# The third mixer of a two-network kernel, rearranged by head group

## What is computed

```python
def fox_attention(q, k, v, logf):                  # 16 heads of 64, 256 tokens
    c = jnp.cumsum(logf, axis=1).transpose(0, 2, 1)
    for i in range(nb):                            # two blocks of 128 queries
        lo, hi = i * blk, (i + 1) * blk
        s = einsum('bqhd,bkhd->bhqk', q[:, lo:hi], k[:, :hi]) * scale
        s = s + c[:, :, lo:hi, None] - c[:, :, None, :hi]
        p = softmax(where(causal, s, NEG_INF))
        outs.append(einsum('bhqk,bkhd->bqhd', p, v[:, :hi]))

def fox_mixer(h, w_in, b_f, w_out):
    q, k, v, fl = split(h @ w_in, [1024, 2048, 3072])   # fl: one logit a head
    logf = log_sigmoid(fl + b_f)
    return fox_attention(q, k, v, logf) @ w_out
```

## Time and profile before

| what | us |
|---|---|
| median of 3 timed runs (1780.7 to 1783.34) | 1781.23 |
| the profiled execution's own time | 1790.02 |
| its span, first to last instruction | 1788.3 |
| PE busy in the span | 1709.6 (96%) |
| DVE, ACT, POOL busy | 1080.5, 802.1, 163.6 |
| mixer: first product of the columns to first of the output product | 1434.01 to 1554.62 |

### The profile page before, as it was taken

The page is one execution under the profiler, slowest core; times in us unless marked ns, Lnnn a source line. Parts: engine busy times, 40 slices in busy tenths (PEclk is TensorE's granted clock), DMA queues, the critical chain, the costliest instruction groups (busy, mean ns, idle before and its releaser), DMA issues.

```text
span 1788.3 us, 31012 instructions
## 1 busy us (share of the span) xinstructions
PE 1709.6 (96%) x13150; PEld 1641.2 (92%) x13150; DVE 1080.5 (60%) x1060; ACT 802.1 (45%) x935; POOL 163.6 (9%) x123
## 2 busy tenths in 40 slices
PE   7999998999999999999999998889999999789997
PEld 7999985899999999989999998669999998689997
DVE  6564776465567664686556876555655566556553
ACT  5343557444346443464434544345444544444442
POOL 1000123100003000030000342110000000100000
PEclk9999999999999999999999998779999999999999
DMA  7544451164543644446454353003554525125550
GB/s 275 210 171 181 165 190 68 50 257 150 210 156 129 258 169 183 180 161 241 153 199 168 137 200 142 1 24 119 189 177 176 211 83 201 47 96 192 185 188 24
DMA packets 39636, 282.33 MB, mean 158 GB/s; under 512 B 4416, under 2 KB 4544, under 8 KB 5760
## 3 DMA queue, kind: packets, MB, share of 16 engines
q1 hardware_dynamic: 39168, 279.59, 42.2%
q0 software_dynamic: 384, 1.51, 0.2%
HBM read 280.03 MB, written 1.05 MB: 157 GB/s over the span
## 4 chain that ended last, share of the span: by engine, by line
PE 88%; DVE 5%; ACT 4%; DMA 1%; issue 1%; POOL 1%; SPq 0%; DVEq 0%; ACTq 0%; POOLq 0%
PE ps L308 27%; PE ps L309 27%; PE ps L310 27%; ACT arena L1078 1%; PE ps L662 1%; PE ps L392 1%; PE ps L606 1%; ACT w_hi L894 1%; DVE w_lo L1213 1%; DMA raw<-weights 1%; PE ps L619 1%; PE ps L638 0%; PE ps L663 0%; POOL arena L1825 0%; DVE stat L1523 0%
## 5 line engine op out<-in xcount | busy, mean ns | idle before, releaser
L308 PE MATMUL ps<-hT_hi,w_hi 128*128 128x256 f32 x2520 | 720.8, 286 | 25.5 <-DVE hT_lo L1225 18.9
L309 PE MATMUL ps<-hT_lo,w_hi 128*128 128x256 f32 x2520 | 716.4, 284 | 0.0
L310 PE MATMUL ps<-hT_hi,w_lo 128*128 128x256 f32 x2520 | 716.2, 284 | 0.0
L1213 DVE TENSOR_TENSOR w_lo<-raw,w_hi 128x2048 fp32r<-128x2048 f32 x264 | 601.0, 2299 | 147.1 <-ACT w_hi L894 147.0
L894 ACT ACTIVATE w_hi<-raw 128x2048 fp32r<-128x2048 f32 x264 | 494.7, 1902 | 62.7 <-DMA raw<-weights 50.8
L308 PEld LDWEIGHTS ps<-hT_hi,w_hi 128*128 128x128 f32 x2520 | 486.7, 193 | 28.3 <-DVE w_lo L1213 13.1
L309 PEld LDWEIGHTS ps<-hT_lo,w_hi 128*128 128x128 f32 x2520 | 487.2, 193 | 0.8 <-issue 0.7
L310 PEld LDWEIGHTS ps<-hT_hi,w_lo 128*128 128x128 f32 x2520 | 486.9, 193 | 0.0
L308 PE MATMUL ps<-hid_hi,w_hi 128*128 128x256 f32 x1256 | 356.0, 283 | 2.6 <-DVE hid_lo L1313 2.6
L309 PE MATMUL ps<-hid_lo,w_hi 128*128 128x256 f32 x1256 | 356.6, 284 | 0.0
L310 PE MATMUL ps<-hid_hi,w_lo 128*128 128x256 f32 x1256 | 351.7, 280 | 0.0
(11 more groups left out here) (227 smaller groups left out, 1468.1 us busy)
## 6 DMA issues: line engine op xcount, KB each, us to landing
raw<-weights SPq DMA_DIRECT2D x264, 1024.0 KB, 4.8
X<-x SPq DMA_DIRECT2D x2, 512.0 KB, 7.1
out<-X SPq DMA_DIRECT2D x4, 256.0 KB, 2.1
arena<-p POOLq DMA_DIRECT2D x2, 256.0 KB, 6.0
arena<-counts POOLq DMA_DIRECT2D x1, 512.0 KB, 4.6
arena<-nsa_tables POOLq DMA_DIRECT2D x1, 448.0 KB, 6.9
const<-constants SPq DMA_DIRECT2D x1, 423.0 KB, 10.0
cols<-parameters SPq DMA_DIRECT2D x1, 213.5 KB, 2.6
```

The lines of the kernel that those rows point to most:

```text
L308: nc.tensor.matmul(dst, a_hi, b_hi, start=start, stop=False, skip_group_check=True)
L309: nc.tensor.matmul(dst, a_hi, b_lo, start=False, stop=False, skip_group_check=True)
L310: return nc.tensor.matmul(dst, a_lo, b_hi, start=False, stop=stop, skip_group_check=True)
L1213: nc.vector.tensor_tensor(unit_cols(w_lo, u, 0, UNIT), raw[:, r * UNIT:(r + 1) * UNIT], f(unit_cols(w_hi, u, 0, UNIT)), ALU.subtract).then ...
```

## The change

The units of the mixer come in another order: the logits' unit first, then for each group of four heads one unit of Q, one of K, one of V (256 columns each), then the output product. PE runs them as `unit(0)` to `unit(11)`, each in a bank of its own among 4 to 7. Scores, transposes and weighted sums of a group are put between the products of later units, and those of the last group between products of the output. There is one score buffer now (banks 0 to 2, the transposes use them too) and one bank (3) for a group's result, which is kept aside once (`heads_aside`). V has the tokens stationary and 256 columns moving, in place of 512. ACT and DVE get a hand-written order to match.

The forget table is gone: the logits are laid down twice (rows 0 to 15 and 32 to 47), rows 32 to 63 of `FORGET` become the low half, and one product a head and tile with `PICK` adds both halves at once. Its moving sides are 256 and 128 columns.

```diff
@@ PE: fox @@
-                logits_and_columns(u0)
-                for b in range(1, 4):
-                    columns_t([u0 + 1 + 2 * b, u0 + 2 + 2 * b], mid={1: lambda: sums(s), 5: lambda: spread(7)} if b == 1 else {})
-                columns([u0 + 9, u0 + 10])
...
-                softmax_attention(FOX_JOBS, ..., prologue, v_ready)
-                project(u0 + 13, squares=True)
+                def scores(g):
+                    if g == 0:
+                        pe.wait_ge(*forget_split.due(me))
+                    pe.wait_ge(qk_taken.sem, 2 * g + 2)
+                    for s in range(HG):
+                        h = HG * g + SLOT_HEAD[s]
+                        pick = PICK[:, h:h + 1].broadcast_to((P, P))
+                        nc.tensor.matmul(A(0, s, 0, 256), pick, FORGET, start=s % 2 == 0, stop=False, skip_group_check=True)
+                        nc.tensor.matmul(bank(2, s * P, P), pick, FORGET[:, 0:P], start=s == 0, stop=False, skip_group_check=True)
...
+                def output(u):
+                    for k in range(KC):
+                        if k % 2 == 0:
+                            pe.wait_ge(hT_ready.sem, heads_before + k // 2 + 1)
+                        for m in range(KC):
+                            if (k, m) == (3, 6):
+                                transposed(3)
+                            elif (k, m) == (4, 3):
+                                weighted(3)
...
+                logits_and_first()
+                unit(1, {2: lambda: sums(s), 6: lambda: spread(7)})
+                unit(2, {7: forget_columns})
+                unit(3, {1: lambda: scores(0)})
+                unit(4)
+                unit(5, {4: lambda: transposed(0), 6: lambda: weighted(0), 7: lambda: scores(1)})
+                unit(6)
+                unit(7)
+                unit(8, {2: lambda: transposed(1), 4: lambda: weighted(1), 5: lambda: scores(2)})
+                unit(9)
+                unit(10)
+                unit(11, {0: lambda: transposed(2), 2: lambda: weighted(2), 3: lambda: scores(3)})
+                hT_ready.due(me, GROUPS)
+                pe.wait_ge(qk_taken.sem, 2 * GROUPS)
+                pe.wait_ge(v_taken.sem, GROUPS)
+                output(u0 + 13)
@@ ACT: fox, in its new order @@
+                split_to(u0 + 9)
+                values(0)
+                split_to(u0 + 10)
+                exponentials()
+                split_to(u0 + 12)
+                copy_transposed()
+                values(1)
+                heads_high(0)
+                split_to(u0 + 13)
+                exponentials()
+                split_to(u0 + 15)
+                copy_transposed()
+                values(2)
+                heads_aside()
...
+                copy_transposed()
+                split_to(u0 + 18)
+                values(3)
+                heads_high(1)
+                heads_high(2)
+                exponentials()
+                split_to(u0 + 19)
+                copy_transposed()
+                heads_high(3)
@@ DVE: fox, its first two groups @@
+                split_to(u0 + 8)
+                masked_scores(0)
+                columns_taken(3)
+                split_to(u0 + 10)
+                weights()
+                columns_taken(4)
+                copy_transposed()
+                split_to(u0 + 12)
+                heads_low(0)
+                masked_scores(1)
+                columns_taken(6)
+                split_to(u0 + 13)
+                weights()
+                columns_taken(7)
+                copy_transposed()
```

More of the change, by code:

```diff
@@ L81 @@
 NTABLE = 2 * TOKENS + 3 * P
-FOX_JOBS = [(g, "fox") for g in range(GROUPS)]
 NSA_JOBS = [(g, b) for g in range(GROUPS) for b in ("slc", "win", "cmp")]
@@ L141, in network_kernel @@
         cols = sb("cols", NCOLS)
-        stat = sb("stat", 192)
+        stat = sb("stat", 160)
         spare = sb("spare", 512)
@@ L207, in pooled_chunk, with heads_chunk @@
             return chunk(h, 2 * g + c, n) if g < 2 else chunk(hid, 2 * (g - 2) + c, n)
+        def heads_chunk(hid, h, k, n=1):
+            return chunk(hid if k < 2 else h, k, n)
         def lhs(t, c, tok):
@@ new lines, in fox, with values @@
+                act.wait_ge(*c_ready.due(me))
+                nc.scalar.activation(FORGET, MINUS_C, ACT.Copy).then_inc(forget_hi.sem, 1)
+                def values(g):
+                    act.wait_ge(unit_used.sem, u0 + 4 + 3 * g)
+                    for tok in range(TT):
+                        ins = nc.scalar.activation(at(QKV + 4096 + tok * DM + g * 256, 256), bank(4 + (3 * g + 2) % 4, tok * 256, 256), ACT.Copy, scale=rstd[:, tok:tok + 1])
+                    ins.then_inc(v_taken.sem, 1)
@@ new lines, in exponentials @@
+                def exponentials():
+                    act.wait_ge(*max_ready.due(me))
+                    for s in range(HG):
+                        for qt in range(TT):
+                            e = at(s * 256, 256) if qt else at(1024 + s * P, P)
+                            c, to = qt * HG + s, qt * HG + SLOT_HEAD[s]
+                            ins = nc.scalar.activation(e, e, ACT.Exp, bias=nmax[:, c:c + 1], accum_out=rsum[:, to:to + 1])
+                    ins.then_inc(p_done.sem, 1)
@@ new lines, in copy_transposed, with heads_high, heads_aside @@
+                def copy_transposed():
+                    act.wait_ge(*t_full.due(me))
+                    nc.scalar.activation(at(3072, 1024), ps[:, 0:1024], ACT.Copy).then_inc(tA_done.sem, 1)
+                def heads_high(g):
+                    if g != 1:
+                        act.wait_ge(*hT_full.due(me))
+                    nc.scalar.activation(heads_chunk(hid_hi, hT_hi, 2 * g, 2), HEADS_1 if g == 1 else bank(3), ACT.Copy).then_inc(hT_hi_done.sem, 1)
+                def heads_aside():
+                    act.wait_ge(*hT_full.due(me))
+                    nc.scalar.activation(HEADS_1, bank(3), ACT.Copy).then_inc(aside_done.sem, 1)
+                    act.wait_ge(*aside_done.due(me))
@@ L1570, in fox, with columns_taken, masked_scores @@
             def fox(s, u0):
+                def columns_taken(i):
+                    g, part = divmod(i, 3)
+                    dve.wait_ge(unit_used.sem, u0 + 2 + i)
+                    times_rstd(at((QT, KT)[part] + g * 512, 512), bank(4 + i % 4), None if part else QSCALE).then_inc(qk_taken.sem, 1)
+                def masked_scores(g):
+                    dve.wait_ge(*s_full.due(me))
+                    for s in range(HG):
+                        h = HG * g + SLOT_HEAD[s]
+                        nc.vector.scalar_tensor_tensor(at(s * 256, 256), A(0, s, 0, 256), cq[:, HEADS + h:HEADS + h + 1], K("mask"), ALU.add, ALU.add)
+                        ins = nc.vector.scalar_tensor_tensor(at(1024 + s * P, P), bank(2, s * P, P), cq[:, h:h + 1], K("mask", P, P), ALU.add, ALU.add)
+                    step(ins)
+                    nc.vector.tensor_reduce(nmax[:, 0:HG], at(1024, 512).rearrange("p (h k) -> p h k", h=HG), AX.X, ALU.max, negate=True)
+                    nc.vector.tensor_reduce(nmax[:, HG:2 * HG], at(0, 1024).rearrange("p (h k) -> p h k", h=HG), AX.X, ALU.max, negate=True).then_inc(max_ready.sem, 1)
@@ L1600, in nsa @@
+                heads_low(1)
+                heads_low(2)
+                split_to(u0 + 18)
+                weights()
+                copy_transposed()
+                heads_low(3)
             def nsa(s, u0):
```

253 lines of the change are left out of this document (151 added, 102 removed).

## The result

The changed kernel takes 1769.99 us (median of 4 timed runs, 1767.18 to 1772.11), against 1781.2 us in the same comparison: ratio 0.9931, 95% interval 0.9908 to 0.9954. It is 11.2 us faster; the prediction was 1768.6 us. Two more comparisons of the same kernel gave 1769.45 (ratio 0.9923, 0.9900 to 0.9946) and 1769.29 (0.9920, 0.9900 to 0.9940).

What follows compares the result with a forecast made beforehand. PE, busy 96% of the span, was taken as the bound. 74.5 + 1.3 + 14.8 + 13.8 + 0.7 + 2.9 = 108.0 us of mixer against 120.6, so 12.6 less: 1768.6 us from 1781.2, range 1764.8 to 1773.8.

Steps and rivals of the forecast that it cites:

- scores, a group: Scores on PE: 2.70 + 0.92 + 0.1 for the way in = 3.7 us a group, four groups 14.8 us.
- new waits: PE's waits for softmax chains, ACT's copy and values ahead of the output: 0.7, 0.4, 0.5, 0.1, 1.15, together 2.9 us.
- hand-overs: PE's returns from tile work to weight products: some 0.1 us each, seven times, 0.7 us.
- Attention between products: Attention after the last column: placing tile work between weight products removes 12.4 us of PE's idle time and slow clock.
- rival 1: Softmax chains at groups 0 to 2 do not fit: 6 us lost, saving 6.6, 1774.6 us; chance 0.15.
- Forget products: Scores on PE: 0.12 us for each forget product of 256 columns, 0.11 for 128, 0.92 us a group.
- Rival 2: Forget products cost least and the new waits vanish: saving 16.3 us, 1764.9 us; chance 0.07.
- Narrow V: V columns on PE: 192 products of 256 columns take 23.0 us where 96 of 512 took 22.1, 0.9 more.
- The start: Mixer's start on PE: first 25 products 5.45 us at low clock, then 0.12 each, no wait for incoming chunks.
- Rival 3: Clock falls at hand-overs, 2.45 us each: four falls 1778.4 us, twelve 1798.0; with rival 4, 0.04 near-zero, 0.04 slower.
- Rival 4: Weight streaming falls behind; 6 us late each is slower by 11; with rival 3, 0.04 near-zero, 0.04 slower.
- Behind the output: After the output product nothing changes: the norm, the MLP and its units find the same conditions.

Runs made afterwards that it cites:

- experiments 3 and 4: Changed kernel with weighted sums right behind the transposes (3): 1775.56 us; with group 1's transposes and weighted sums one unit sooner (4): 1777.83 us.
- after: The changed kernel, first comparison and its profile: timed median 1769.99 us, profiled execution 1772.11 us.
- after_again: The changed kernel once more, timed and profiled against the kernel before: 1769.45 us, ratio 0.9923.
- experiment 2: The kernel before, with the third mixer's two V blocks computed with 256 moving columns in place of 512: 1783.45 us, ratio 1.0017.
- before: The kernel before the change, in its first profile: profiled execution 1790.0 us, timed median 1781.2 us.
- early_group1: Changed kernel with group 1's transposes and weighted sums in unit 7 in place of unit 8: 1777.83 us, ratio 0.9983.
- forget_alone: The kernel before with only the new forget bias, one product a head and tile in place of the table: 1780.32 us, ratio 0.9993.
- experiment 6: Three versions of the changed kernel: later wait for the last values; also a second unit in the first block; also later hand-overs: 1769.79, 1768.44, 1768.46 us.
- no_short: The changed kernel without the forget products of 128 columns: 1768.93 us, ratio 0.9941.
- late_v: Changed kernel with the wait for the last values moved behind the first 18 output products: 1769.79 us, ratio 0.9935.
- before_again: The kernel before, timed against itself and profiled once more: 1781.03 us, ratio 0.9984.
- two_first: Changed kernel with the later wait for the last values and a second unit of columns in the first block: 1768.44 us, ratio 0.9928.
- best: Changed kernel with later wait for last values, second unit in first block, and groups 0 and 1 handed over one chunk later: 1768.46 us, ratio 0.9916.

## Why the prediction was right

The forecast was a saving of 12.6 us in the mixer, and the timed saving was 11.2, 11.8 and 13.1 us in three comparisons. The mechanism is the one forecast, shown by experiments 3 and 4. That the number came out within 1.4 us is in part luck: terms set too high and too low made up for each other. From the mixer's first product to the output's, 104.4 us were forecast, for a start at half clock. Measured are 102.66 in after (full clock) and 103.3 in after_again (half clock, 1430.20 to 1533.49). By step:

| term | forecast | measured in after |
|---|---|---|
| first 72 products | 5.45 + 47 x 0.12 = 11.1 | 10.2 (to 1440.75) |
| other 528 products | 0.12 each, 63.4 | 60 take 7.20: 0.12 each |
| sums, spread, small transposes | 1.3 | 0.44 + 0.36 + 0.23 = 1.0 |
| scores, a group | 3.7, 0.1 of it for the way in | 3.65, without the way in |
| transposes, weighted sums, a group | 1.3 + 2.15 | 1.26 + 2.15 |
| new waits | 2.9 | 0.3 + 0.26 + 0.07 + 1.13 = 1.8 |
| hand-overs | 0.4 to 0.5 in this stretch | 1.5, what is left |

- **Attention between products.** Right. The 12.4 us of idle and slow clock are gone, the clock is at 1.00, and no wait for a softmax is longer than 0.3 us. Experiments 3 and 4 show it from the other side: take the cover away and 6 to 8 us come back.
- **The new waits** were set too high, 2.9 for 1.8. The single prices stood (POOL 2.40, exponentials 3.5, copy 1.0), and so did the wait before the output, 1.15 for 1.1. The estimates erred at the ACT copy of group 0 (0.4 forecast, none seen) and by 0.4 and 0.2 us at groups 0 and 1 (0.7 and 0.5 forecast). There is no margin at groups 0 to 2, and the wait of group 0 reached 0.5 to 0.8 us in other versions. That shows how near rival 1 lay: one unit of distance less costs 8 us.
- **Hand-overs** were set too low, 0.5 for 1.5, nearly as much as the waits were too high. The price of a return was right and their number wrong. In after's timeline the second weight product behind a step starts 0.20 to 0.22 us after the first, where a stream has 0.12: 0.08 to 0.10 us for each return, 0.1 forecast. But thirteen returns lie in the stretch, where the forecast has seven in the whole mixer. The way in costs 0.09 us at the small transposes and at each of the weighted sums (0.21 in place of 0.12) and nothing at transposes or scores that need not wait (0.12), where the forecast had 0.1 for the scores. Thirteen returns and four ways in come to 1.5 us.
- **Forget products.** 0.11 us was taken for 128 columns, 0.10 is measured. Rival 2 is out, in this part as in its waits.
- **Narrow V.** 0.9 us was set down; 1.17 measured at the third weighted sums in experiment 2.
- **The start.** The argument that the chunks cost no wait held for the half clock, for which it was made. At the full clock it fails: PE stands 0.32 us at each of the last four chunks. The forecast took one profiled execution's start for the kernel's. The kernels differ there: at half clock the mixer saves 142.43 - 128.59 = 13.8 us, with the fall of some 3 us 141.78 - 127.88 = 13.9, at full clock about (15.91 + 124.14) - 127.95 = 12.1, where 124.14 is the part of before's mixer behind the sums. The 12.6 were worked out for the half clock, so they are 1.2 us short of their own case; which starts the timed executions had is not on record.
- **Rival 3**, the clock falling at hand-overs, did not come: twelve insertions and pauses of up to 1.0 us left it at 1.00. Behind longer pauses it was down: 5.86 us in early_group1, 2.01 in forget_alone.
- **Rival 4** did not come either: no line of PE's waits in after names a unit's load or half. A trace of it is there, through ACT: a load that lands 0.4 to 0.6 us later makes group 0 wait longer (experiment 6).
- **Behind the output** nothing was to change: 211.86 and 211.90 us.

## What to carry to other kernels

Where one engine is the bound and a chain over the other engines makes it wait, look for independent products to place inside the chain, and cost each hop with its hand-overs: the chain here has nothing to spare, and one unit of distance less costs more than two thirds of the gain. Count every return to the stream, and check whether what one edit saves is waited for at the next place (no_short at group 0). A wait that grows ahead of an edit is not its work: compare from a place behind it (late_v). Before the sizes of two profiled executions are subtracted, cut them at places that the edit does not touch: here 3.5 of 17.9 us lay outside it.

## What the hardware did that was not expected

- The clock at one and the same place differs from execution to execution of the same kernel. After the norm, before the mixer, the changed kernel was seen at full clock throughout, at half from the first product, and at half for 3 us from some 2 us on. Further up it is alike: between 1100 and 1200 us the granted clock was 0.71 in before, 0.81 in before_again, and in after:

```profile
1100.00:1200.00 100.00, 82.01 (x467) 67.19 (x465) 60.30 (x116) 44.80 (x153) 19.19 (x8) 0.78 0.07 27
```

  The mixer's start moved with it in these three: 1434.01, 1427.83, 1430.55 us. Over all thirteen profiles it lies between 1427.00 and 1434.04 with equal code ahead of the mixer. The clock is part of the reason and not all of it: at the same mean of 0.81 two_first starts at 1429.02 and no_short at 1427.00.
- Behind the mixer it differs too. At the norm there PE pauses 1.0 and 2.25 us, and the clock was at half for 3.4 us in most profiles, but for 6.8 in best and no_short; what follows the mixer then took 213.0 and 212.7 us in place of 211.9. Their profiled times contain that.
- Pauses of PE of 1.0 to 1.5 us inside the mixer did not bring the clock down; behind one of 2.01 us, and behind those of 4.92, 5.86 and 6.52, it was down. By the pauses of 1.1 and 2.25 us ahead of the mixer it fell in 7 of 13 executions.
- A forget product of 128 columns costs 0.10 us, one of 256 columns in a stream 0.12.
